# Second stack: the attention results are split for the output projection inside the attention, and the last unit is finished under the projection's first lot

## The reference

```
proj = rmsnorm(x, norm_attn) @ w_in
o_sb, o_mb, o_ns, o_df = stick-breaking, block-selected, three-branch and differential attention, 4 heads each
mixed = concat(o_sb, o_mb, o_ns, o_df)             # 512 x 1024
x = x + mixed @ w_out                              # 1024 x 1024
x = x + square(relu(rmsnorm(x, norm_mlp) @ w_up)) @ w_down
```

## Time and profile before

| what | value |
|---|---|
| median of 3 runs | 3185.42 us (3185.02 to 3190.41) |
| profiled execution, its own time | 3191.14 us |
| profiled execution, its span | 3189.3 us |
| PE busy | 2917.1 us, 91% |
| DVE, ACT, POOL busy | 1445.4, 1070.5, 235.5 us |
| mean granted PE clock | 0.929 |
| attention, layer 1 of the second stack | about 2597 to 2767 us |
| its output projection | about 2767 to 2822 us |

### The profile page before, as it was taken

The page is one execution under the profiler, slowest core; times in us unless marked ns, Lnnn a source line. Parts: engine busy times, 40 slices in busy tenths (PEclk is TensorE's granted clock), DMA queues, the critical chain, the costliest instruction groups (busy, mean ns, idle before and its releaser), DMA issues. The chain is left out here.

```text
span 3189.3 us, 48320 instructions
## 1 busy us (share of the span) xinstructions
PE 2917.1 (91%) x18362; PEld 2513.4 (79%) x18362; DVE 1445.4 (45%) x2292; ACT 1070.5 (34%) x1482; POOL 235.5 (7%) x206
## 2 busy tenths in 40 slices
PE   7897899989899789989898888999989888899998
PEld 6886899988897789989788545788868864578886
DVE  3732477722663267762332454433433245443342
ACT  3234434322233443322322233432332223343232
POOL 1000300010100120001100012000010001200000
PEclk9988999999998899999898788999999878899999
DMA  3200322222220132222321001223223200022322
GB/s 129 85 22 14 125 92 79 84 82 72 85 77 4 40 126 92 81 80 89 117 104 67 27 1 40 80 92 105 93 87 104 80 27 1 22 84 92 102 96 105
DMA packets 44799, 238.08 MB, mean 75 GB/s; under 512 B 4894, under 2 KB 14750, under 8 KB 21360
## 3 DMA queue, kind: packets, MB, share of 16 engines
q1 hardware_dynamic: 34976, 223.04, 20.3%
q10 hardware_dynamic: 9680, 13.16, 1.2%
HBM read 234.03 MB, written 11.59 MB: 77 GB/s over the span
## 5 line engine op out<-in xcount | busy, mean ns | idle before, releaser
L156 PE MATMUL psum<-u_up_a_hi,w_a_hi 128*128 128x264 f32 x1408 | 378.3, 289 | 19.2 <-DVE u_up_a_lo L1702 15.8
L157 PE MATMUL psum<-u_up_a_lo,w_a_hi 128*128 128x264 f32 x1408 | 374.2, 286 | 0.0
L147 DVE TENSOR_TENSOR w_mlp_b_lo<-ring,w_mlp_b_hi 128x1024 fp32r<-128x1024 f32 x128 | 156.8, 1225 | 332.7 <-ACT w_mlp_b_hi L140 332.7
L147 DVE TENSOR_TENSOR w_a_lo<-ring,w_a_hi 128x1024 fp32r<-128x1024 f32 x150 | 183.9, 1227 | 245.0 <-ACT w_a_hi L140 242.6
L156 PEld LDWEIGHTS psum<-u_up_a_hi,w_a_hi 128*128 128x128 f32 x1408 | 266.0, 189 | 27.0 <-DVE u_up_a_lo L1702 19.6
L159 PE MATMUL psum<-u_up_a_hi,w_a_lo 128*128 128x264 f32 x1408 | 286.8, 285 | 0.0
L157 PEld LDWEIGHTS psum<-u_up_a_lo,w_a_hi 128*128 128x128 f32 x1408 | 265.5, 189 | 0.3
L140 ACT ACTIVATE w_a_hi<-ring 128x1024 fp32r<-128x1024 f32 x150 | 158.3, 1057 | 313.4 <-PE psum L159 308.0
L140 ACT ACTIVATE w_mlp_b_hi<-ring 128x1024 fp32r<-128x1024 f32 x128 | 136.1, 1064 | 301.5 <-PE psum L159 300.7
L159 PEld LDWEIGHTS psum<-u_up_a_hi,w_a_lo 128*128 128x128 f32 x1408 | 220.2, 189 | 0.0
L156 PE MATMUL psum<-u_up_b_hi,w_mlp_b_hi 128*128 128x512 f32 x512 | 201.5, 394 | 9.7 <-DVE u_up_b_lo L586 9.7
(11 more groups left out here) (414 smaller groups left out, 6638.3 us busy)
## 6 DMA issues: line engine op xcount, KB each, us to landing
ring<-in_wup SPq DMA_DIRECT2D x44, 1024.0 KB, 4.7
ring<-in_wup_b SPq DMA_DIRECT2D x32, 1024.0 KB, 4.8
ring<-in_wdown_b SPq DMA_DIRECT2D x32, 1024.0 KB, 4.8
ring<-in_win SPq DMA_DIRECT2D x22, 1024.0 KB, 4.8
ring<-in_wdown SPq DMA_DIRECT2D x32, 704.0 KB, 4.1
ring<-in_win_b SPq DMA_DIRECT2D x12, 1024.0 KB, 4.9
near_copies<-near_rows ACTq DMA_DIRECT2D x2, 4608.0 KB
ring<-in_wout SPq DMA_DIRECT2D x8, 1024.0 KB, 4.7
```

Source lines behind the costliest of these rows:

```text
L147: nc.vector.tensor_tensor(W["lo"][:, buf, 0:n], W["tiles"][:, slot, at:at + n], W["hi"][:, buf, 0:n].bitcast(F32), ALU.subtract).then_inc( ...
L156: nc.tensor.matmul(out[c], a_hi, b_hi, start=start, stop=False)
L157: nc.tensor.matmul(out[c], a_hi, b_lo, start=False, stop=False)
```

## The change

In `attend_stage_b`:

- ACT rounds five tiles of y early, in the order `EARLY_Y` = 0, 1, 2, 3, 6: the first four after step 1 of units 4 to 7, y6 after step 3 of unit 8. The places in `fm` that they go to are no longer read by then, and waits on `mixed` guard that.
- POOL makes their low parts, each after the finish of the same unit, with a wait for ACT's copy.
- The finish of unit 9 is taken out: DVE's copy, ACT's logarithm and exponential, POOL's three operations.

In `out_stage_b`:

- ACT, after the first lot's weights, takes the logarithm and the exponential, rounds y7 and y4 (`LATE_Y` = 7, 4, 5), rounds the second lot's weights, and rounds y5 when it is complete.
- DVE, after the first lot's low weights, multiplies PSUM bank 6 by the inverted sums, makes the low parts of y7 and y4, multiplies by the gate, adds to y5, makes the second lot's low weights, and then the low part of y5. POOL has only the sum of squares left.
- PE takes the tiles in the order 0, 1, 2, 3, 6, 7, 4, 5 in every lot, and waits in lot 0 for the last three only.

`crossed`, `at_sums` and `at_part_y` stay allocated through the projection; the attention's other buffers are freed.

```diff
 def products_b(nc, pe, S, W, layer, L):
-            for k in range(KD):
-                if L.fresh is not None and j == 0:
-                    pe.wait_ge(L.fresh[k % 2].sem, L.fresh[k % 2].at(layer, k // 2 + 1))
+            for k in L.order:
+                if L.fresh is not None and j == 0 and k in L.fresh:
+                    made, count = L.fresh[k]
+                    pe.wait_ge(made.sem, made.at(layer, count))
 def out_stage_b
         def _(act):
             high_of(nc, act, W, layer, L, 0, 0)
-            for k in range(KD):
-                nc.scalar.activation(parts[0][:, k, :], y[:, k, :], ACT.Copy).then_inc(S["y_high"].sem, 1)
-                if k == 3:
-                    high_of(nc, act, W, layer, L, 0, 1)
+            nc.scalar.activation(sums[:, :], ps[:, 7, :], ACT.Ln).then_inc(last_logged.sem, 1)
+            act.wait_ge(last_logged.sem, last_logged.at(layer, 1))
+            nc.scalar.activation(sums[:, :], sums[:, :], ACT.Exp, scale=-1.0).then_inc(last_inverted.sem, 1)
+            for k in LATE_Y[0:2]:
+                high(k)
+            high_of(nc, act, W, layer, L, 0, 1)
+            act.wait_ge(last_mixed.sem, last_mixed.at(layer, 3))
+            high(LATE_Y[2])
 def attend_stage_b, ACT
+                    if n in range(4, 8) and step == 1:
+                        early_high(n - 4)
+                    if (n, step) == (8, 3):
+                        early_high(4)
                 if n + 1 < U:
                     rows_of_maxima(n + 1)
-                log_sums(n)
-            invert(U - 1)
+                    log_sums(n)
 DVE
-            copy_mixed(U - 1)
+            pass_waits(dve, S)
 POOL
-            for n, u in enumerate(UNITS_B):
+            for n, u in enumerate(UNITS_B[:-1]):
...
+                if n >= 4:
+                    k = EARLY_Y[n - 4]
+                    pool.wait_ge(S["early_high"].sem, S["early_high"].at(layer, n - 3))
+                    nc.gpsimd.tensor_tensor(fm[1][:, k, :], y[:, k, :], fm[0][:, k, :].bitcast(F32), ALU.subtract)
```

More of the change, by code:

```diff
@@ L329 @@
     stats: int | None = None
-    fresh: tuple | None = None
+    fresh: dict | None = None
+    order: tuple = tuple(range(KD))
     needs: tuple | None = None
@@ L499, in relu_vector_b, with out_stage_b @@
     in_rounds(dve, L.rounds(), step)
-def out_stage_b(nc, S, W, layer, L, y, parts, h):
+def out_stage_b(nc, S, W, layer, L, M, y, parts, h):
+    ps, sums, part_y, gate = S["psum"], M["sums"], M["part_y"], M["gate"]
+    y_high, y_low, last_logged, last_inverted, last_mixed = (
+        S[x] for x in ("y_high", "y_low", "last_logged", "last_inverted", "last_mixed"))
+    u = UNITS_B[-1]
     with nc.Block() as block:
@@ L516, in _, with high @@
         def _(act):
+            def high(k):
+                nc.scalar.activation(parts[0][:, k, :], y[:, k, :], ACT.Copy).then_inc(y_high.sem, 1)
             high_of(nc, act, W, layer, L, 0, 0)
-            for k in range(KD):
-                nc.scalar.activation(parts[0][:, k, :], y[:, k, :], ACT.Copy).then_inc(S["y_high"].sem, 1)
-                if k == 3:
-                    high_of(nc, act, W, layer, L, 0, 1)
+            nc.scalar.activation(sums[:, :], ps[:, 7, :], ACT.Ln).then_inc(last_logged.sem, 1)
[6 more added lines that the diff above has]
+            high(LATE_Y[2])
             add_scalar_b(nc, act, S, W, layer, L, h)
@@ L525, in _, with low @@
         def _(dve):
+            def low(i):
+                dve.wait_ge(y_high.sem, y_high.at(layer, i + 1))
+                nc.vector.tensor_tensor(parts[1][:, LATE_Y[i], :], y[:, LATE_Y[i], :], parts[0][:, LATE_Y[i], :].bitcast(F32),
+                                        ALU.subtract).then_inc(y_low.sem, 1)
             dve.sem_inc(S[L.free].sem, L.tiles())
             low_of(nc, dve, W, layer, L, 0, 0)
[L528 to L532, removed]
+            dve.wait_ge(last_inverted.sem, last_inverted.at(layer, 1))
+            nc.vector.tensor_tensor(part_y[:, :], ps[:, 6, :], sums[:, :], ALU.mult).then_inc(last_mixed.sem, 1)
+            low(0)
+            low(1)
+            dve.wait_ge(last_mixed.sem, last_mixed.at(layer, 1))
+            nc.vector.tensor_tensor(part_y[:, :], part_y[:, :], gate[:, u["gate"], :], ALU.mult).then_inc(last_mixed.sem, 1)
+            dve.wait_ge(last_mixed.sem, last_mixed.at(layer, 2))
+            nc.vector.tensor_tensor(y[:, u["y"], :], y[:, u["y"], :], part_y[:, :], ALU.add).then_inc(last_mixed.sem, 1)
             low_of(nc, dve, W, layer, L, 0, 1)
+            low(2)
             add_vector_b(nc, dve, S, W, layer, L, h)
@@ L3029, in mixer @@
                 L = Product(lambda j: A["wout_b"][layer, j], 4, parts, 16, 54, 24, 0, lambda j: A["wup_b"][layer, j],
-                            stats=0, fresh=S["y_low"])
-                out_stage_b(nc, S, W, layer, L, y, parts, h)
+                            stats=0, fresh={k: (S["y_low"], i + 1) for i, k in enumerate(LATE_Y)}, order=EARLY_Y + LATE_Y)
+                out_stage_b(nc, S, W, layer, L, M, y, parts, h)
         def mlp(layer, scope):
@@ L3038, in mlp @@
             ups = [Product(lambda j: A["wup_b"][layer, j], 8, u, 20, 62, 32, 0, lambda j: A["wdown_b"][layer, j],
-                           ready=True, ahead=28, fresh=S["u_low"], free="up_free"),
+                           ready=True, ahead=28, fresh={k: (S["u_low"][k % 2], k // 2 + 1) for k in range(KD)}, free="up_free"),
                    Product(lambda j: A["wup_b"][layer, j + 8], 8, u, 36, 94, 64, 16, lambda j: A["wdown_b"][layer, j + 8],
```

52 lines of the change are left out of this document (31 added, 21 removed).

## The result

The changed kernel takes 3160.4 us at the median of 8 runs (3153.4 to 3174.2). The kernel before, on the same chip, takes 3185.2 us (8 runs, 3177.6 to 3190.4). The ratio is 0.9925, 95% interval 0.9906 to 0.9943: faster by 24.9 us. The forecast was 14.0 us, and the time lies 6.1 us under the range given (3166.5 to 3180).

The account below looks back on a forecast made before the run. PE, busy 91% of the span, was taken as the bound, so time cut from its pauses counts: 2 x (7.0 + 0 + 0 + 0) = 14.0 us, 3185.42 - 14.0 = 3171.4 us. Range for 8 in 10: 3166.5 to 3180.

Parts of the forecast that it names:

- The pause: PE's idle time between attention and projection: 2.95 instead of 9.97 us, 7.0 us saved per layer, ends 7.3 and 6.5.
- The barrier: Between attention and projection: ACT starts the first weights 0.58 us after PE's end, ends 0.27 and 1.05.
- the weights' chain: At the projection's start: from ACT's first weights to PE's start 2.37 us instead of 4.05.
- The wait changed its name: Sign at the projection's start: PE's wait on `fm_lo` goes, one on `w_out_b_lo` of about 2.9 comes in each layer.
- The late tiles: Projection's lot 0: PE's stall for y7, y4, y5 taken as 0 per layer, ends 0 and 0.6 us.
- DVE's product from PSUM: Sign in the projection: DVE's product from PSUM bank 6 stands about 2.3 us after the first weights.
- y5's low part: Projection's lot 0: ready at 7.8 us, wanted at 7.2 at full clock, a stall of 0.6; none at half clock.
- The attention: Added ACT copies and POOL subtractions in the attention cost 0, as they are covered; far end 2.3 us per layer.
- The clock: PE's half clock behind the projection's pause: change taken as 0 per layer, ends +0.4 and -1.0 us.
- the clock that stays up: Rival: no fall of PE's clock behind the projection's pause; gain 8.4 us per layer, time 3168.6, chance 0.08.
- the first of the four subtractions: DVE's low parts at the projection's start: only the first, 1.7 us, is on the path and counted in the pause.
- the spread of three runs: Whole kernel: the runs before spread over 5.4 us, which with the forecast's own range gave some 3167 to 3178.

Follow-up runs that it names:

- e2: The changed kernel again, without an edit, with a new profile: 3161.3 us, 0.9939 to the kernel before.
- e6: The changed kernel with the projection's tiles in the order 0 to 7 instead of the late ones last: 3168.7 us, 0.9952 to the kernel before.
- e1: The kernel before, unchanged, against itself, with a new profile: 3187.8 us, 1.002.
- e9: The kernel before with unused dummy products of PE in the pause, ten ahead of the barrier and seven behind it: 3177.1 us, 0.9970 to the kernel before.
- e5: The changed kernel with four dummy products of PE in the pause, result not used: 3160.5 us, 0.9926 to the kernel before.
- e11: The changed kernel with four unused dummy products of PE in the pause, run in a later set: 3160.2 us, 0.9914 to the kernel before.
- e7: The changed kernel with ACT's logarithm and exponential ahead of the first lot's weights: 3173.6 us, 0.9963 to the kernel before.
- e8: The changed kernel with the first lot's weights split during the attention: 3166.2 us, 0.9941 to the kernel before.
- e12: The changed kernel with the first lot's weights split during the attention, run in a later set: 3167.0 us, 0.9936 to the kernel before.

## Why the prediction was wrong

**The pause: right.** It got shorter by 7.15 instead of 7.0 per layer. The barrier took 0.46 (0.58 forecast), the weights' chain 2.36 (2.37). The wait changed its name as said.

**The late tiles: right.** DVE's product from PSUM stood 2.23 after the first weights (2.3 forecast). y5's low part was ready at 2746.82 + 0.68 = 2747.50, that is 7.18 after ACT's first weights (7.8 forecast). PE does not wait in lot 0 of the changed kernel, in e2 at full clock neither: five tiles and y7 and y4 keep it busy for 21 x 0.228 = 4.8 us, until 7.15 after the first weights: within 0.03 the cover is used up. e6 shows that it is real: with another order PE waits 1.2.

**The attention: right, and its cover held where it was named.** Unit 7 in layer 1, two profiles of the same pattern: DVE's small maximum, ACT's exponent behind it and PE's product, first the kernel before (e1), then the changed one (e2) with the new subtraction on POOL:

```profile
2712.19 0.16 DVE L2725 TENSOR_TENSOR top<-top 128x4 f32<-128x4 f32 x1
...
2713.00 0.60 ACT L2622 ACTIVATE at_prob<-psum 128x512 f32<-128x512 f32 x1 [2.39 <-DVE psum L2757]
2715.04 1.98 PE L2532 MATMUL psum<-at_prob,v_tm 128*64 128x256 f32 x8
```

```profile
2700.52 1.28 POOL L2956 TENSOR_TENSOR fm_lo<-y_b,fm_hi 128x512 fp32r<-128x512 f32 x1
2700.74 1.08 DVE L2764 TENSOR_TENSOR top<-top 128x4 f32<-128x4 f32 x1
...
2702.46 0.60 ACT L2644 ACTIVATE at_prob<-psum 128x512 f32<-128x512 f32 x1 [3.31 <-DVE psum L2796]
2703.58 1.98 PE L2554 MATMUL psum<-at_prob,v_tm 128*64 128x256 f32 x8
```

The maximum went from 0.16 to 1.08 under the subtraction. Counted from the attention's start (2606.17 and 2594.80) the exponent comes at 107.66 instead of 106.83, and PE's product at 108.78 instead of 108.87: covered, as worked out. The attention without the pause takes what it took (0.12 less in this layer). The scaling of y7 went from 0.74 to 1.20, also without a wait of PE. This is the lock between DVE and POOL that the prediction took from the Trainium skill, "SBUF — State Buffer", section "Who interferes with whom": the trace agrees, and the cover decided that it costs nothing.

**The clock: the step that failed.** The prediction set this term to 0, with ends of -1.0 and +0.4, mainly from one row: that the clock would fall behind a pause of 2.95, since it had fallen behind 2.87. It gave 0.08 to the clock that stays up. In fact a pause of 2.82 goes either way, and like for like the projection gets shorter by 53.9 - 51.8 = 2.1 us per layer in one pattern and by some 0.5 to 1.3 in the other (53.8 and 54.6 to 53.3). The second is near the forecast's end of +0.4, and six of the eight profiled layers had it. The rival's own size was off as well: it charged 0.6 for y5, which was on time (7.18, not 7.8). Its 8.4 per layer should have been 7.15 + 2.1 = 9.3, and the time 3166.8 by the sum of the prediction. That still lies in the range: this step alone doesn't bring the time to 3160.4.

**A second cause of that, hidden before.** The prediction counted only the first of the four subtractions as being on the path. At full clock the other three pace PE, 0.9 us per layer (e9); of the 2.1 that the projection gained at full clock, only 1.2 is the clock, and 0.9 is that the change took these subtractions out of PE's way. That the rival's 2.0 for the clock comes so near the 2.1 is luck: it counted matmuls at half clock without this pace.

**The size of the measurement.** The first comparison's 24.9 us hold 14.3 of the pause and up to 4.2 of the projection. The rest is 6 us or more. The two profiles of that comparison differ by 15.2 us in code that both kernels share, 9.2 of it ahead of layer 0's stick-breaking. That is more than enough for the 6; that the other runs got them there too is argued, as they have no trace. This is the second term that failed: the prediction took the spread of three runs, 5.4 us, for that of the kernel, and gave no room for it below 3166.5. 20 timed executions of the changed kernel lie between 3153 and 3177, and the kernel before differs from itself by 8 us between two sets of runs (e1). Three sets gave 24.9, 18.7 and 21.1 us, whose intervals overlap between 18 and 27 us. The forecast's 14.0 is outside the first and just inside the other two.

**What stays open.** What a run does not show is why one execution takes one pattern and another the other. e9's 9.6 us (6.4 to 13) are more than its stages explain (4.4), and e7 loses more than its stages show. Both may come from a shift of when later stages fall against the clock's changes, which I did not test. That the filled kernel (e5, e11) is better than the changed one is not shown either: none of its 12 runs is above 3166 us, and five of the changed kernel's 20 are above 3168, but the intervals overlap.

## What to carry to other kernels

Price a pause of TensorE with two terms: its length, and what runs at half clock behind it. Here the stage behind gained up to 2.1 us on 7.15. For a pause close in length to one that was followed by a fall, both outcomes have to be given real chances; one row is not a verdict. Before a single number for the clock is believed, compare the stages that the change does not touch: where they differ by more than the term in question, only pairs of profiles with the same pattern can tell its size.

When half clock hides a pace (here a pair of tiles each 1.69 us against 1.37), mending the clock alone gives less than it should: 1.2 us of the projection, where mending both gave 2.1.

A filler is tested only where the clock would have fallen without it. Four filled layers at full clock say nothing if the unfilled kernel keeps its clock in the same pattern.

## What the runs showed that I had not expected

- The same pause of 2.82 us, at full clock on both ends, was followed by full clock in e2 (22 matmuls in 5.00 us) and by 3.4 us of half clock, 1.42 us after the restart, in the first profile of the changed kernel. After 3.82 us (e7) it fell in both layers, both of the pattern in which it stays up behind 2.82. After 0.8 us (e8, e12) it fell in none of four, two of them of the pattern in which it falls behind 2.82.
- The attention of one program takes 148.2 or 151.5 us, stick-breaking 67.6 to 76.8, with the same instructions, by where the clock falls in it. All that lies ahead of it, 1721 to 1731 us in these profiles, varies too.
- A `Block` barrier with PE last costs ACT 0.46 and POOL 0.29 us from PE's end to their first operation.
